# Activation tiles and weight slots each moved 64 bytes on, modulo 512, from their neighbour

## The reference

```
h = h + 0.5 * swiglu(rmsnorm(h), w_gate, w_up, w_down)      # 1024 -> 2816 -> 1024
n = rmsnorm(h) @ w_in   -> sliding-window attention and gated linear attention
h = h + concat(attn_o, gla_o) @ w_out
h = h + 0.5 * swiglu(rmsnorm(h), ...)
h = h + sigmoid(rmsnorm(h) @ ple_w_gate) * rmsnorm(p @ ple_w_proj)
# second block, two layers
even layer: short conv and differential attention;  odd layer: stick-breaking attention
after each: cross-attention into 256 memory tokens, then a gated MLP with a width-3 conv
```

## Time and profile before

| | |
|---|---|
| time of a run, two runs | 2563.40 and 2562.87 us, median 2563.14 |
| span of the profiled execution | 2561.3 us |
| what lies around the span, by the two runs | 1.6 to 2.1 us |
| TensorE busy | 2541.6 us, 12548 matmuls |
| VectorE busy | 1596.4 us |
| ScalarE busy | 912.6 us |
| granted TensorE clock, mean | 1.000 |

### The profile page before, as it was taken

The page is one execution under the profiler, slowest core; times in us unless marked ns, Lnnn a source line. Parts: engine busy times, 40 slices in busy tenths (PEclk is TensorE's granted clock), DMA queues, the critical chain, the costliest instruction groups (busy, mean ns, idle before and its releaser), DMA issues.

```text
span 2561.3 us, 31974 instructions
## 1 busy us (share of the span) xinstructions
PE 2541.6 (99%) x12548; PEld 2107.0 (82%) x12548; DVE 1596.4 (62%) x1976; ACT 912.6 (36%) x1184; POOL 10.2 (0%) x24
## 2 busy tenths in 40 slices
PE   8999999999999999999999999999999999999999
PEld 7888888778888888877898888888886888888887
DVE  6444468866444468677765747476357665775755
ACT  5222234543222245344443423233146343432322
POOL 0000001000000000000000000000000000000000
PEclk9999999999999999999999999999999999999999
DMA  5222233112222232212321232323210232232222
GB/s 182 102 83 99 96 110 120 67 50 96 103 89 98 99 115 101 99 50 99 132 94 63 104 103 82 115 83 123 94 66 13 87 116 83 84 115 83 101 96 82
DMA packets 37410, 241.91 MB, mean 94 GB/s; under 512 B 4416, under 2 KB 7280, under 8 KB 9136
## 3 DMA queue, kind: packets, MB, share of 16 engines
q1 hardware_dynamic: 34736, 233.78, 26.3%
q10 hardware_dynamic: 1920, 5.22, 0.6%
q0 software_dynamic: 640, 1.31, 0.2%
HBM read 236.89 MB, written 2.10 MB: 93 GB/s over the span
## 4 chain that ended last, share of the span: by engine, by line
PE 93%; DVE 5%; ACT 1%; issue 1%; DMA 0%; POOL 0%; DVEq 0%; ACTq 0%
PE ps L605 24%; PE ps L607 24%; PE ps L606 24%; PE ps L1234 1%; PE ps L623 1%; PE ps L625 1%; PE ps L624 1%; PE ps L766 1%; PE ps L1267 1%; PE ps L1291 1%; PE ps L1282 1%; DVE w_lo L2048 1%; PE ps L768 1%; PE ps L767 1%; PE ps L1303 1%
## 5 line engine op out<-in xcount | busy, mean ns | idle before, releaser
L605 PE MATMUL ps<-op_hi,w_hi 128*128 128x512 f32 x2056 | 800.9, 390 | 0.2 <-DVE op_lo L1929 0.2
L606 PE MATMUL ps<-op_lo,w_hi 128*128 128x512 f32 x2056 | 800.5, 389 | 0.0
L607 PE MATMUL ps<-op_hi,w_lo 128*128 128x512 f32 x2056 | 800.4, 389 | 0.0
L1350 ACT ACTIVATE w_hi<-w_raw 128x2048 fp32r<-128x2048 f32 x217 | 414.4, 1911 | 485.2 <-PE ps L607 315.3
L2048 DVE TENSOR_TENSOR w_lo<-w_raw,w_hi 128x2048 fp32r<-128x2048 f32 x217 | 497.0, 2292 | 38.7 <-ACT w_hi L1350 22.3
L605 PEld LDWEIGHTS ps<-op_hi,w_hi 128*128 128x128 f32 x2056 | 386.3, 188 | 81.4 <-issue 1.4
L607 PEld LDWEIGHTS ps<-op_hi,w_lo 128*128 128x128 f32 x2056 | 386.2, 188 | 80.6
L606 PEld LDWEIGHTS ps<-op_lo,w_hi 128*128 128x128 f32 x2056 | 386.3, 188 | 80.3
L2013 DVE SCALAR_TENSOR_TENSOR x<-ps,x 128x512 f32<-128x512 f32 x134 | 92.7, 691 | 310.8 <-PE ps L607 293.0
L605 PE MATMUL ps<-h_hi,w_hi 128*128 128x512 f32 x692 | 269.5, 389 | 0.0
L606 PE MATMUL ps<-h_lo,w_hi 128*128 128x512 f32 x692 | 269.2, 389 | 0.0
(11 more groups left out here) (373 smaller groups left out, 3085.7 us busy)
## 6 DMA issues: line engine op xcount, KB each, us to landing
w_raw<-in_wstream_dram SPq DMA_DIRECT2D x217, 1024.0 KB, 4.8
cr_m<-in_mem_dram ACTq DMA_DIRECT2D x2, 1024.0 KB, 4.9
w_raw<-in_wstream_dram SPq DMA_DIRECT2D x7, 256.0 KB, 8.0
x<-in_x_dram SPq DMA_DIRECT2D x3, 512.0 KB, 7.3
out_dram<-x SPq DMA_DIRECT2D x3, 512.0 KB, 2.6
m_s<-m_q POOLq DMA_DIRECT2D x16, 64.0 KB, 2.5
ev_s<-in_alibi_dram ACTq DMA_DIRECT2D x1, 1024.0 KB, 4.9
m_c<-in_rope_dram ACTq DMA_DIRECT2D x1, 640.0 KB, 3.9
```

The costliest lines, as they stand in the source:

```text
L605: mm_(o, w_hi[:, c % 4, w], hi[:, k, 0:cols], start=(k == 0), stop=False)
L606: mm_(o, w_hi[:, c % 4, w], lo[:, k, 0:cols], start=False, stop=False)
L607: mm = mm_(o, w_lo[:, c % 4, w], hi[:, k, 0:cols], start=False, stop=(k == kt - 1))
L1350: f_(w_hi[:, c % 4, :], w_raw[:, c % 2, :], ACT.Copy).then_inc(w_hi_ready, 1)
```

## The change

Between neighbouring activation tiles in `op_hi` and `op_lo`, and between neighbouring slots in `w_hi` and `w_lo`, 16 unused elements (64 bytes) are put, so tile k begins 64k bytes and slot c begins 64c bytes further modulo 512 than tile or slot 0. The instructions use the same 512 or 2048 elements of each as before. Two unused tensors of 256 bytes fill each weight tensor up to a multiple of 512 bytes. The four paddings with the fills take 2048 bytes a partition, and the scratch at address 0 is made 8192 bytes instead of 16384. `h_hi`, `h_lo` and all other tensors keep their shapes.

```diff
--- before.py
+++ after.py
@@ -55,6 +55,7 @@
 AT_CONV1 = AT_CROSS1 + CROSS_SLABS + DOWN
 SLABS = AT_CONV1 + MLP_SLABS
 PIECES = 4
+STEP = 16
 
 
 
@@ -166,10 +167,12 @@
             od_lo = sb("od_lo", [P, 2, TRI], FP32R, s)
             od_hi = sb("od_hi", [P, 2, TRI], FP32R, s)
 
-        op_hi = sb("op_hi", [P, KT, SEQ], FP32R)
-        op_lo = sb("op_lo", [P, KT, SEQ], FP32R)
-        w_hi = sb("w_hi", [P, 4, SLAB], FP32R)
-        w_lo = sb("w_lo", [P, 4, SLAB], FP32R)
+        op_hi = sb("op_hi", [P, KT, SEQ + STEP], FP32R)[:, :, 0:SEQ]
+        op_lo = sb("op_lo", [P, KT, SEQ + STEP], FP32R)[:, :, 0:SEQ]
+        w_hi = sb("w_hi", [P, 4, SLAB + STEP], FP32R)[:, :, 0:SLAB]
+        sb("fill_hi", [P, 4 * STEP])
+        w_lo = sb("w_lo", [P, 4, SLAB + STEP], FP32R)[:, :, 0:SLAB]
+        sb("fill_lo", [P, 4 * STEP])
 
         with ExitStack() as s:
             h_hi = sb("h_hi", [P, 8, SEQ], FP32R, s)
@@ -2956,7 +2959,8 @@
     import concourse.bacc as _bacc
     from concourse.bass_utils import run_bass_kernel_spmd as _run
 
-    nc = _bacc.Bacc("TRN2", target_bir_lowering=False, num_devices=1)
+    nc = _bacc.Bacc("TRN2", target_bir_lowering=False, num_devices=1,
+                    dynamic_dma_scratch_size=8192)
     arrays, args = {}, {}
     for name, a in lay_out({k: np.asarray(v) for k, v in inputs.items()}).items():
         arrays[f"in_{name}_dram"] = np.ascontiguousarray(a)
```

## The result

The changed kernel takes 2602.9 us (two runs, 2601.96 and 2603.77) against 2563.1 before: ratio **1.0157**, 95% interval 1.0141 to 1.0174. It is 39.7 us slower. The profiled execution's span grew from 2561.3 to 2600.2 us, by 38.9 us, so the trace holds nearly the whole loss. In the changed kernel the lines are numbered 3 higher: L605 to L607 are L608 to L610, L2048 is L2051.

A forecast was written before the change was run, and what follows sets the result against it. TensorE's matmul start-to-start step, 226.7 ns, was taken to bound the kernel. All terms were taken as 0 us on the profiled span of 2561.3, giving 2563 us against the median 2563.1; range 2486 to 2597.

The forecast's parts named there:

- What bounds the kernel: TensorE, busy 99% of the span: time set by matmul start-to-start distance, 226.7 ns, times their number.
- the 64-byte beat: Wide matmuls: moving stream served in 64-byte steps on a fixed beat, so multiples of 64 B cost 0 ns.
- the prediction's last paragraph: Signs to check; forecast wrong if the beat is longer than 64 B in address, unexcluded for offsets 64, 128, 192.
- a lost beat: Slower rival, wide matmuls: one beat more; on half the pairs 2593 (chance 0.06), on all 2623 (0.09).
- price of 35 beats for every wide matmul: Slower rival on all 9,048 wide matmuls: +6.67 ns each, +60 us, 2623; chance 0.09.
- term for the 256-column matmuls: 768 matmuls with weights moving at L623: taken as 0, between -2.4 and +5.1 us.
- only the odd multiples of 64 B are bad: Slower rival on half the pairs of wide matmuls: +30 us, 2593; chance 0.06.
- The faster rivals: Wide matmuls: one beat faster 2518 (0.10); full excess undone on new relations 2488 (0.10), on all 2464 (0.07).
- The 11 ns above L1195's step: Wide matmuls: 226.7 against L1195's 215.7 ns, the most an address edit could gain; 99.5 us in all.
- the upper bound, +6.7 ns at offset 288: Wide matmuls: worst loss per step, taken from the embeddings' 48 matmuls at 233.5 ns.
- scratch 0: Half the scratch, affecting only POOL's copies: taken as 0, +40 us if uncovered; no chance of its own.
- the shift by a common amount 0: All later tensors move down together by 6144 B, twelve times 512; relations stay, 0.

The follow-up runs named there:

- run 2: Weight slots alone padded by 64 B, scratch halved, against the kernel before: 2593.7 us, ratio 1.0123.
- run 3: Activation tiles alone padded by 64 B, scratch halved, against the kernel before: 2594.1 us, ratio 1.0128.
- run 5: Weight slots alone padded by 448 B, scratch halved, against the kernel before: 2591.7 us, ratio 1.0116.
- run 4: Activation tiles alone padded by 512 B, scratch halved, against the kernel before: 2562.1 us, ratio 0.9999.
- run 6: Weight slots alone padded by 256 B without fills, scratch halved, against the kernel before: 2562.5 us, ratio 1.0002.
- run 9: Weight slots alone padded by 80 B, scratch halved, against the kernel before: 2588.4 us, ratio 1.0103.
- run 11: Weight slots alone padded by 144 B, scratch halved, against the kernel before: 2583.6 us, ratio 1.0085.
- run 8: Weight slots alone padded by 16 B, scratch halved, against the kernel before: 2591.9 us, ratio 1.0116.
- run 1: Scratch alone halved, no padding, against the kernel before: 2562.2 us, ratio 1.0001.
- run 7: A 32 B tensor put ahead of all others, scratch halved, against the kernel before: 2562.3 us, ratio 1.0001.
- run 15: Only w_lo moved 64 B on, no padding between slots, scratch halved, against the kernel before: 2598.0 us, ratio 1.0140.

## Why the prediction was wrong

**What bounds the kernel** was right: the step between matmuls on a TensorE that never waits. After the change the chain and the clock are as before, and the longer step explains the loss.

**The step that failed is the one on the 64-byte beat.** The prediction said that every offset of the change "is a multiple of 64" and that "seen from such a beat tile 1 looks like tile 0 one beat later", and took 0 ns for the wide matmuls. Runs 2, 3 and 5 show 229 to 233 ns at 64, 128 and 192 B. The relation between stream and load repeats after 256 B (runs 4 to 6), not 64. I had one multiple of 64 in the old trace, 256, and read from it that all multiples are harmless; it is the only harmless one of the kind, being the period itself. Nor do the other offsets have to lose: 16 and 112 B, and 240 B in one of its two patterns, keep 226.7 to 226.9 ns (runs 9, 11 and 8). The lengths told the beat in time. That it is the period in address too was an inference, and the prediction's last paragraph named it as what would make it wrong.

**What was right in it:** that relative addresses act at all: 226.7 against 233.3 ns for the same instructions, with only the offset changed. The Trainium skill's "TensorE: Matmul & The Clock Gate", section "Step-by-step: what each phase is for", says that loading the next tile's weights takes no SBUF read bandwidth from the running matmul. If that meant that the two never touch, the offset could not act, and the trace doesn't agree with that.

**The rivals.** The slower one, a lost beat, is what happened, at a price between its two forms (2593 and 2623). My price of 35 beats for every wide matmul was too high. In the first MLP the hidden tiles' four slots mean 230.6 ns, +3.9, and op tiles are at 232, +5.3, in every slot. The tiles k whose offset is 0 don't get back to 226.7 either: in run 3, k = 0 and k = 4 (offsets 0 and 256) are at 230 ns, since six matmuls are too few to settle again, which takes about eight. At these two prices 6,936 and 2,112 matmuls would be +45 us. Over the whole trace it is less: +30.7 us for the 6,168 on op tiles and +7.6 for the 2,076 on hidden tiles at L608 to L610, and only +2.2 for the other 804, many of which stand between other work and weren't settled before. The prediction's term for the 256-column matmuls, 0 within -2.4 to +5.1 us, held with -1.6. The same kind of matmul with `cr_mhi` and `cr_mlo`, +0.8, was in none of its terms. The form "only the odd multiples of 64 B are bad" was wrong: 128 costs 5.8 ns.

**The faster rivals** fell at every multiple of 16 B. The 11 ns above L1195's step are not undone by any offset tried. What they are stays open; that L1195's 256 plain float32 columns are the same work as 512 of fp32r, on which the 11 ns rest, no run shows either.

**The range** ended at 2597, because I had left the full lost beat (2623, 0.09) out of it and priced the half one at 2593. The rows that I used for the upper bound, +6.7 ns at offset 288 and eight slower steps after a single foreign one, should have weighed more than a mechanism inferred from ratios: they were the only measured cases of a changed offset with 512 columns, and every one but 256 was slower.

**The rest** was right: scratch 0 (run 1), the shift by a common amount 0 (runs 1 and 7), ScalarE and VectorE 0 (1,909 and 2,292 ns after).

**Left open:** what makes the 32 cycles of the settled step; why two patterns exist at -16; and whether the load beside is the partner (three changes of slot speak for it, run 15 doesn't tell).

## What to carry to other kernels

Measure the step from matmul start to matmul start, not the duration, and look whether it is constant: in this kernel, which is little but load and stream, a steady 226/227 is a settled pattern that one foreign address broke for eight matmuls (for a whole slab in run 8), and a changing address for good. For fp32r matmuls of 512 columns, keep the moving tiles and the weight tiles at one and the same start modulo 256 B, across all tensors that take turns. Where a trace has only a few values of a quantity, test a period with the value between them before building on it.

## What the runs showed of the hardware

The settled steps lie on one grid. By the starts in full, every run of twelve or more settled matmuls in the trace of before, over 2.5 ms and through all stalls between them, falls within 0.25 ns of one grid of 6.67 ns, once a drift of 1.6 parts in a million is taken out (35 runs, 8,448 steps). From this I infer that the settling is to something that runs on through the stalls, and not only to the matmul before. The steady steps are 34 units each (226.7) or turns that add up to 35 a matmul (233.3), or other turns, such as 103 units for three matmuls (229, 232 and 226 ns, mean 229.0).

The pattern's price depends on the width. For 256 columns the settled step is the longer one (120.0 against 117 ns), for 512 the shorter, so that the same padding gained 1.6 us in L626 to L628, where the mean step without pauses fell from 119.6 to 118.2 ns, and lost 38.3 in L608 to L610.
